# First of the four weight sums of an MLP down unit: made by transfers of GpSimd's queue in place of VectorE

## What is computed

```
def sq_relu_mlp(h, w_up, w_down):
    return jnp.square(jax.nn.relu(h @ w_up)) @ w_down

def second_block(x, p, norm_g, ...):
    for i in range(DEPTH_2):
        ...
        f = sq_relu_mlp(rmsnorm_2(x, g[2]), w_mlp_up[i], w_mlp_down[i])
        x = x + rmsnorm_2(f, g[3])
        ...
```

## Time and profile before

| | us |
|---|---|
| median of three timed executions | 1722.89 |
| lowest and highest of them | 1721.89, 1722.9 |
| the profiled execution's time | 1720.62 |
| its span | 1718.8 |
| TensorE busy (share of the span) | 1701.4 (99%) |
| VectorE busy | 1197.6 (70%) |
| ScalarE busy | 918.7 (53%) |
| GpSimd busy | 169.8 (10%) |
| granted TensorE clock, mean | 0.998 |

### The profile page before, as it was taken

The page is one execution under the profiler, slowest core; times in us unless marked ns, Lnnn a source line. Parts: engine busy times, 40 slices in busy tenths (PEclk is TensorE's granted clock), DMA queues, the critical chain, the costliest instruction groups (busy, mean ns, idle before and its releaser), DMA issues.

```text
span 1718.8 us, 24363 instructions
## 1 busy us (share of the span) xinstructions
PE 1701.4 (99%) x9127; PEld 1453.1 (85%) x9127; DVE 1197.6 (70%) x1845; ACT 918.7 (53%) x1544; POOL 169.8 (10%) x147
## 2 busy tenths in 40 slices
PE   9999999999999999999999999999999999999998
PEld 7888877888778897889898988878887999998977
DVE  6378877776566777587585976775566848587866
ACT  4267874665436667466445454652235746354555
POOL 2011212000300000220000002320003000000041
PEclk9999999999999999999999999999999999999999
DMA  8222123214233322223242423323322332424321
GB/s 271 82 72 74 45 72 97 74 50 147 74 87 90 83 75 80 74 74 123 74 126 71 145 66 121 91 69 100 116 91 74 99 123 74 123 74 123 111 74 50
DMA packets 147133, 160.65 MB, mean 93 GB/s; under 512 B 13929, under 2 KB 121990, under 8 KB 146774
## 3 DMA queue, kind: packets, MB, share of 16 engines
q1 hardware_dynamic: 146870, 159.19, 29.7%
q10 hardware_dynamic: 160, 0.07, 0.0%
HBM read 150.43 MB, written 4.19 MB: 90 GB/s over the span
## 4 chain that ended last, share of the span: by engine, by line
PE 96%; DVE 2%; ACT 2%; issue 0%; DVEq 0%; ACTq 0%
PE bank L1030 29%; PE bank L1031 29%; PE bank L1032 29%; PE bank L1367 2%; PE bank L1391 1%; PE bank L1288 1%; PE bank L1277 1%; DVE act_a L2441 0%; PE bank L1662 0%; ACT act_a L1759 0%; DVE work L2472 0%; PE bank L1203 0%; PE bank L1187 0%; PE bank L1312 0%; PE bank L1219 0%
## 5 line engine op out<-in xcount | busy, mean ns | idle before, releaser
L1030 PE MATMUL bank<-act_a,split_weights 128*128 128x512 f32 (+1 forms) x1400 | 550.7, 393 | 4.5 <-DVE act_a L2439 2.0
L1032 PE MATMUL bank<-act_a,split_weights 128*128 128x512 f32 (+1 forms) x1400 | 544.2, 389 | 0.0
L1031 PE MATMUL bank<-act_a,split_weights 128*128 128x512 f32 (+1 forms) x1400 | 543.7, 388 | 0.0
L1030 PEld LDWEIGHTS bank<-act_a,split_weights 128*128 128x128 f32 x1400 | 262.5, 187 | 62.0 <-issue 4.4
L1032 PEld LDWEIGHTS bank<-act_a,split_weights 128*128 128x128 f32 x1400 | 262.2, 187 | 56.1
L1031 PEld LDWEIGHTS bank<-act_a,split_weights 128*128 128x128 f32 x1400 | 262.6, 188 | 51.1 <-issue 0.2
L2381 DVE TENSOR_TENSOR split_weights<-raw_weights,split_weights 128x2048 fp32r<-128x2048 f32 x68 | 156.9, 2307 | 148.8 <-ACT split_weights L1704 135.8
L1704 ACT ACTIVATE split_weights<-raw_weights 128x2048 fp32r<-128x2048 f32 x64 | 122.2, 1909 | 198.5 <-PE bank L1032 198.4
L1030 PE MATMUL bank<-act_b,split_weights 128*128 128x256 f32 (+1 forms) x648 | 207.1, 320 | 0.0
L1032 PE MATMUL bank<-act_b,split_weights 128*128 128x256 f32 (+1 forms) x648 | 206.4, 318 | 0.0
L1031 PE MATMUL bank<-act_b,split_weights 128*128 128x256 f32 (+1 forms) x648 | 206.3, 318 | 0.0
(11 more groups left out here) (313 smaller groups left out, 2941.5 us busy)
## 6 DMA issues: line engine op xcount, KB each, us to landing
raw_weights<-in_w_mlp_up SPq DMA_DIRECT2D x32, 1024.0 KB, 5.5
raw_weights<-in_w_mlp_down SPq DMA_DIRECT2D x32, 1024.0 KB, 5.0
raw_weights<-in_w_in SPq DMA_DIRECT2D x18, 1024.0 KB, 5.3
raw_weights<-in_w_conv_in SPq DMA_DIRECT2D x12, 1024.0 KB, 5.2
raw_weights<-in_w_attn_in SPq DMA_DIRECT2D x16, 512.0 KB, 4.8
raw_weights<-in_w_ple_gate SPq DMA_DIRECT2D x8, 1024.0 KB, 4.9
raw_weights<-in_w_out SPq DMA_DIRECT2D x4, 1024.0 KB, 4.9
raw_weights<-in_w_attn_in SPq DMA_DIRECT2D x4, 1024.0 KB, 5.3
```

Source lines behind the costliest of these rows:

```text
L1030: nc.tensor.matmul(dst, w[0], a[0], start=first, stop=False)
L1031: nc.tensor.matmul(dst, w[0], a[1], start=False, stop=False)
L1032: mm = nc.tensor.matmul(dst, w[1], a[0], start=False, stop=last)
```

## The change

s1 is no longer made by VectorE. GpSimd's program gets a part, `first_weight_sums`, between its sums of squares. For each down unit it issues two transfers that copy w(1,0) from HBM into `sums[0]` (`sum_begun`), waits for both, and issues two that read w(1,1) from HBM and add it to what lies in `sums[0]` (`accum_op=ALU.add`, `sum_loaded`). Each moves 128 partitions x 2 x 128 elements, 128 KB. For every unit but the first it waits first until the third product of the unit before is split and that unit's second sum is made. The buffers change places (`SUMMED`): the first sum holds `sums[0]` alone, the fourth overwrites `sums[1]`, so it waits for the fourth product of its unit. The `z` steps stand one place later.

```
-        SUMMED = {2: (0, 1), 3: (1, 2), 4: (0, 4), 5: (2, 3)}
+        SUMMED = {2: (0, 0), 3: (1, 1), 4: (1, 3), 5: (2, 2)}
...
-        DVE_DOWN = ("S2 p14 p15 {a0} p16 {a1} z2 p17 {a2} p18 {a3} p19 {a4} p20 {a5} S3 p21 {a6} p22 p23 z3 "
...
+        DVE_DOWN = ("S2 p14 p15 {a0} p16 {a1} p17 z2 {a2} p18 {a3} p19 {a4} p20 {a5} S3 p21 {a6} p22 p23 "
...
+                    elif i == 2:
+                        act.wait_ge(sum_loaded, 32 * (down_unit_number(layer, c, d) + 1))
                     elif i in SUMMED:
-                        act.wait_ge(sum_made, 4 * down_unit_number(layer, c, d) + SUMMED[i][1])
+                        act.wait_ge(sum_made, 3 * down_unit_number(layer, c, d) + SUMMED[i][1])
...
                     dve.wait_ge(raw_landed[pl.slot], pl.landed)
-                    V.tensor_tensor(s1, weight_part(pl, 1, 0), weight_part(pl, 1, 1), ALU.add).then_inc(sum_made, 1)
                     V.tensor_tensor(s3, weight_part(pl, 0, 0), weight_part(pl, 1, 0), ALU.subtract).then_inc(sum_made, 1)
-                    dve.wait_ge(sum_made, made + 1)
+                    dve.wait_ge(sum_loaded, 32 * (down_unit_number(layer, c, d) + 1))
                     V.tensor_tensor(s2, s1, weight_part(pl, 0, 0), ALU.subtract).then_inc(sum_made, 1)
...
-                    dve.wait_ge(sum_made, 4 * down_unit_number(layer, c, d) + 3)
-                    dve.wait_ge(prod_split, (PRODUCTS - 1) * down_unit_number(layer, c, d) + 3)
-                    V.tensor_tensor(by_blocks(sums[:, 0, :]), weight_part(pl, 0, 1), by_blocks(sums[:, 2, :]), ALU.subtract)\
+                    dve.wait_ge(sum_made, 3 * down_unit_number(layer, c, d) + 2)
+                    dve.wait_ge(prod_split, (PRODUCTS - 1) * down_unit_number(layer, c, d) + 4)
+                    V.tensor_tensor(by_blocks(sums[:, 1, :]), weight_part(pl, 0, 1), by_blocks(sums[:, 2, :]), ALU.subtract)\
...
+            def first_weight_sums(layer):
...
+                pool.wait_ge(tile_done, tab.tile[tab.first[name]] + 1)
+                for c in range(MLP_CHUNKS):
+                    for d in range(4 if c < LAST else 2):
...
+                        if number:
+                            pool.wait_ge(prod_split, (PRODUCTS - 1) * (number - 1) + 3)
+                            pool.wait_ge(sum_made, 3 * (number - 1) + 2)
+                        for h in range(2):
+                            if h:
+                                pool.wait_ge(sum_begun, 32 * (number + 1))
+                            for a in range(2):
...
+                                if h == 0:
+                                    nc.gpsimd.dma_start(dst, rows).then_inc(sum_begun, 16)
+                                else:
+                                    nc.gpsimd.dma_start(dst, rows, accum_op=ALU.add).then_inc(sum_loaded, 16)
```

More of the change, by code:

```diff
@@ L346, in hybrid_block_kernel @@
         sum_made = sem("sum_made")
+        sum_begun = sem("sum_begun")
+        sum_loaded = sem("sum_loaded")
         prod_hi = sem("prod_hi")
@@ L653, in hybrid_block_kernel @@
                    "U2 s0 b0 t0 v0 " + ACT_UP + "k0 c0 c1 c2 j0 q0 q1 q2 q3 n0 q4 q5 q6 q7")
-        DVE_UP = ("T0 b0 y0 t0 v0 U3 T1 b1 y1 t1 v1 S0 p0 p1 p2 z0 p3 T2 b2 y2 t2 v2 p4 p5 p6 S1 p7 T3 b3 y3 p8 t3 p9 v3 z1 "
-                  "p10 p11 p12 p13 ")
-        DVE_DOWN = ("S2 p14 p15 {a0} p16 {a1} z2 p17 {a2} p18 {a3} p19 {a4} p20 {a5} S3 p21 {a6} p22 p23 z3 "
-                    "p24 p25 p26 p27 n0 {a7} {a8} n1 {a9} {a10} n2 {a11} {a12} n3 {a13}")
+        DVE_UP = ("T0 b0 y0 t0 v0 U3 T1 b1 y1 t1 v1 S0 p0 p1 p2 p3 z0 T2 b2 y2 t2 v2 p4 p5 p6 S1 p7 T3 b3 y3 p8 t3 p9 v3 "
+                  "p10 z1 p11 p12 p13 ")
+        DVE_DOWN = ("S2 p14 p15 {a0} p16 {a1} p17 z2 {a2} p18 {a3} p19 {a4} p20 {a5} S3 p21 {a6} p22 p23 "
+                    "p24 z3 p25 p26 p27 n0 {a7} {a8} n1 {a9} {a10} n2 {a11} {a12} n3 {a13}")
         DVE_NEXT = DVE_DOWN.replace("{", "").replace("}", "")
@@ L3032, in weight_sums @@
                     pl = Place(tab, name, 8 * c + 4 + d)
-                    made = 4 * down_unit_number(layer, c, d)
                     s1, s3, s2 = (by_blocks(sums[:, k, :]) for k in range(3))
@@ L3372, in sum_mlp_squares @@
                         .then_inc(sq_added, 1)
+            def first_weight_sums(layer):
+                down = ins["w_mlp_down_2"][layer].rearrange("(c a h p) (b m n) -> p c a h b m n", p=P, a=4, h=2, m=2, n=P)
+                name = f"mlp{layer}"
+                pool.wait_ge(tile_done, tab.tile[tab.first[name]] + 1)
+                for c in range(MLP_CHUNKS):
+                    for d in range(4 if c < LAST else 2):
+                        number = down_unit_number(layer, c, d)
+                        o, part = divmod(d, 2)
+                        if number:
[5 more added lines that the diff above has]
+                            for a in range(2):
+                                dst = sums[:, 0, 2 * P * a:2 * P * a + 2 * P].rearrange("p (b n) -> p b n", b=2)
+                                rows = down[:, c, 2 * part + a, h, 2 * o:2 * o + 2, 1, :]
+                                if h == 0:
+                                    nc.gpsimd.dma_start(dst, rows).then_inc(sum_begun, 16)
+                                else:
+                                    nc.gpsimd.dma_start(dst, rows, accum_op=ALU.add).then_inc(sum_loaded, 16)
             for layer in range(2):
@@ L3376, in _ @@
                 sum_squares(KT)
+                first_weight_sums(layer)
                 sum_mlp_squares()
```

## The result

| | us |
|---|---|
| median with the change, four executions | 1814.48 (1812.45 to 1817.12) |
| median before, in the same comparison | 1722.39 |
| ratio | 1.054, interval 1.0524 to 1.0555 |
| span of the profiled execution | 1810.7 (before 1718.8) |

What follows compares the result with a forecast made beforehand. TensorE's own work was taken to bound the kernel. Removed and moved steps counted 0 us; transfers at L = 8.5 us made four chunks 2.2 us late each, 8.8 us: 1722.89 + 8.8 = 1731.7 us, range 1726 to 1761 (with A from 1721.5).

Steps and rivals of the forecast that it cites:

- No gain from VectorE's spare time: 28 additions of 684 ns, 19.1 us of VectorE, removed beside a TensorE that never waits: worth 0 us.
- The moved steps: `z0` to `z3` one product later and sums in other buffers: 0.6 us of 5 us reserve, worth 0 us.
- The place and the formula: Unit 3's bank-emptying `a6` in chunks 1 and 2, `p21` in chunk 0; late by 2L - 14.8 and 2L - 17.5 us.
- L: Time from the third product's low part, which frees `sums[0]`, until `sum_loaded` is full: forecast 8.5 us.
- the first place: Start of unit 2, whose first product needs the bank `a0` empties: L may be 8.7 us before TensorE waits.
- first step: The two copying transfers into `sums[0]`, 256 KB: 2.6 us landing, plus two issues of 0.63 us.
- second step: The two adding transfers, 256 KB beside a weight load in unit 2: 3.4 us landing, plus two issues of 0.63 us.
- My end from above: GpSimd's issue priced like its 32x512 add, 1.54 us: L = 12.2 us and 52 us late.
- wrong in kind: Signs: TensorE waits in a chunk's first two units, ScalarE's third product is awaited, or matmuls get longer.
- A, hidden anyway: Rival: GpSimd's issue costs 0.37 us like SyncE's, L 7.5 us, 1723.7 us, not slower; chance 0.33.
- B, descriptors held up by VectorE: Rival: each issue waits 0.68 us more, L 11.2 us, 40 us late, 1763 us; chance 0.11 with dearer issues.
- C, faster: Rival: VectorE's spare time removes a TensorE wait, at most 1 or 2 us at the edges, 1721 us; chance 0.04.

Runs made afterwards that it cites:

- The second buffer: The changed kernel with the first sum of odd units in `ssum`, so transfers wait for the unit two places ahead: 1721.92 us, ratio 1.0003.
- Order and buffers alone: The changed kernel's order and buffers, but VectorE makes the first sum again and GpSimd issues nothing: 1722.05 us, ratio 1.0003.
- Moving the second sum: The changed kernel with VectorE's second sum moved behind the unit's third product: 1780.6 us, ratio 1.0342.
- the doubled store: The changed kernel with 2048 bytes of each partition for GpSimd's descriptors in place of 1024: 1783.96 us, ratio 1.036.
- four plain copies: The changed kernel with the second pair of transfers copying in place of adding: 1748.74 us, ratio 1.015.
- half the rows: The changed kernel with adding transfers of only one of the two blocks, 64 KB each: 1752.81 us, one execution.
- transfers that nobody waits for: VectorE makes the first sum in the change's order; GpSimd issues the 112 transfers into idle `ssum`, no other engine waiting: 1721.76 us, ratio 1.0005.

## Why the prediction was wrong

**The sign was right, the size was not:** 8.8 us forecast, 92 measured, and the range ended at 1761 us.

**No gain from VectorE's spare time: right.** The second buffer shows it: 15.6 us less work on VectorE, 1.0003 of the time.

**The moved steps: right.** Order and buffers alone are at 1.0003.

**The place and the formula: right, within a sixth.** The sum 4 x (2L - 14.8) + 2 x (2L - 17.5), with 2L read as the two loads that follow one another, gives with the measured L (15.1 + 12.5 in chunk 1) 12.8 us late in that chunk, and TensorE waited there for 10.9 us. Over all six chunks the L of the changed kernel, 12.5 to 15.4 us, give 74.7 us, and TensorE's new waits there are 62.9 us. The formula is thus some 12 us over; that TensorE's slower matmuls between two waits used up part of the lateness would explain it, and is not shown. The new waits are for `work` in chunks 1 and 2 and for `split_weights` in chunk 0, as said. But there are two in each chunk in place of one, since at this L the first place is late too: TensorE waits already at the start of unit 2, for which I had 8.7 us of room. Moving the second sum changed the room, and the time followed.

**L: the term that failed.** I had 8.5 us, it was 14.3 to 15.4 us for the load of units 2 and 12.5 to 14.7 us for that of units 3 (14.4 and 14.7 us in the first chunk 0, where 2L decides as well). I follow the 15.1 us of unit 2 in chunk 1. Its first step was right: 1.5 us to issue and 2.3 us more to land, against 2.6 + 1.26. The second step was forecast at 3.4 + 1.26 = 4.7 us and took 11.0 us (886.22 to 897.22). Of that

- 2.48 us are the issues, twice what I took. A copy costs GpSimd 0.75 us (forecast 0.63), an adding transfer 1.23 us. My end from above, 1.54 us, held both.
- 6.16 us are the gap, which I had no term for: I bounded the price of an issue and never asked whether an issue could be refused. The before kernel sets aside 1024 bytes for descriptors, a number in its last lines, and issues nothing from there. The doubled store takes 30 us off the whole kernel.
- the rest is 2.36 us of landing. With the doubled store, where the gap does not stretch the step, the landing is seen whole: 5.3 us behind the last issue, where I had 3.4 in all. The second pair of the four plain copies lands as late beside a weight load: from the end of its issue at 971.4 us to the second sum at 976.8 us are 5.4 us, and 1.9 us in the next unit, without one. So what I priced too low is the landing beside the load, and not the adding.

So L fell short in three of its terms: the issues (1.5 us in all four), the landing of the adding pair (1.9 us) and the gap (3.1 us, 15.1 against 12.0 with the doubled store). L = 12.2, my end from above, gave 52 us; with the doubled store, at an L of 12.0 us in this place, 62 us were measured. The gap, which the rows could not show, is worth the other 30.

**The clock: not in the sum.** I had counted a microsecond late as a microsecond of time. Waits of 3.9 to 6.8 us brought TensorE's granted clock down to 0.66 in the stretch around and behind one of them, 27.9 us of longer matmuls in all beside 62.9 us of new waits at the down units. It is so in the other runs, read in the same way: 21.9 beside 41.8 us with the doubled store, 11.7 beside 18.7 us with four plain copies. By my own sign ("wrong in kind ... if its matmuls themselves get longer") this is a step missing from the mechanism, and not only a size.

**A reading.** What I gave as ten waits of TensorE, about 10 us together, is ten kinds of wait, 13 waits, 8.8 us together, and one of them (1.1 us, at the kernel's start) does name `split_weights`. None lies in the MLPs, so nothing hung on it.

**Rivals.** A, hidden anyway, would have needed an issue of 0.45 us at my landing times; it was 0.75 and 1.23. B, descriptors held up by VectorE: GpSimd's issues of one kind are all of a length, whether VectorE is idle or full, as this row of the change shows (ns, shortest, median and longest of 56):

```profile
L3395 POOL DMA_DIRECT2D sums<-in_w_mlp_down x56: 745/754/894, 748.6 to 1690.1; - x56
```

The adding ones took 1.25 us beside a busy VectorE (at 886.22 us) and 1.23 us beside an idle one (at 893.63 us). So B's mechanism did not act, though its L of 11.2 us was nearer than mine. The Trainium skill (SBUF — State Buffer, two separate sides) has GpSimd kept from writing descriptors while VectorE runs in a mode with two ports; the prediction took VectorE's instructions here not to be in it, and the row shows no such hold. The Trainium skill's fit of 2.0 us plus bytes (DMA: Bandwidth & Descriptors, Anatomy of one DMA) gave an estimate of 2.6 us for a step, taken as one transfer of 256 KB; the first step, two copies in line, took 3.8 us (1.5 + 2.3) and the adding one 11.0, so the measurement decides against that estimate here. C, faster, did not occur.

**The signs in the profile.** I had named about 4 us of VectorE's idle time in the third unit and 3 to 4 in the fourth; it was 9.91 and 5.55, under the 11 us set for B. The longer matmuls, named as a sign of being wrong in kind, came. TensorE did not wait in the first two units of a chunk, nor for ScalarE's third product, and weight loads land as before (5.0 us), as said.

## What to carry to other kernels

A step that is moved to a transfer is cheap in traffic and dear in latency: before it is moved, find out how long one round of its buffer is (here 18.2 us from the first transfer of unit 2 to that of unit 3, 882.44 to 900.63, against a pace of 10.03 us a unit), and what stands behind the wait in the queue of the engine that waits. Where the round was longer than the pace here, a second buffer took out the whole loss, and moving the waiting step behind work that did not need it took out over a third. TensorE had no wait to begin with, so freeing VectorE won nothing, and the best form of the change was only even.

## What the runs showed of the hardware

- A transfer of GpSimd's queue that adds into SBUF (128 KB, rows of 512 bytes) costs GpSimd 1.23 us and is 272 packets (median of 56 issues in the changed kernel); the same as a copy costs 0.75 us and is 48 packets (four plain copies).
- With 1024 bytes for descriptors a second such adding transfer is issued 0.33 us after the first has landed, in 28 of 28 units (gaps of 2.5 to 6.4 us); with 2048 bytes, or with half the rows, there is no gap.
- Beside a weight load of 1024 KB the four plain copies of a unit take 3.4 us longer to the step that needs them (10.5 against 7.1 us, one pair of units), while the weight loads land at most 0.2 us later (median, transfers that nobody waits for).
- With a wait of TensorE of 6.50 us up to 899.9 us, its granted clock was 0.66 from 897 to 907 us; from 907 to 917 us, with a second wait of 4.36 us, it was 0.86.
